# Attention of a two-layer block: padded keys, key counts inside the mask, w_out in half rows, squares on two engines

## The reference, cut to what matters

```python
proj = h @ w_in[i]
z, xbc, dt_raw, q, k, v = split(proj)
y_ssd = ssd_mixer(xbc, dt_raw, z, ...)   # ends: y = y * silu(z); y = y * rsqrt(mean(y*y per group of 256)) * ssd_norm
q = rms_norm(q per head, q_norm[i]); k = rms_norm(k per head, k_norm[i])
# three branches, dilation r in (1, 4, 16): query t sees keys t - j*r, j = 0..128
# each branch: softmax over its keys; the branches are mixed by softmax of their log denominators
y_att = dilated_attention(q, k, v)
x = x + concat([y_ssd, y_att]) @ w_out[i]
```

## Time and profile before

| | us |
|---|---|
| median of 3 runs | 2179.38 |
| lowest and highest | 2174.16, 2182.07 |
| the profiled execution | 2182.77 |
| span of its trace | 2180.8 |
| TensorE products busy | 2118.5 (97%) |
| VectorE busy | 1621.4 (74%) |
| ScalarE busy | 1132.8 (52%) |
| GpSimd busy | 441.8 (20%) |

### The profile page before, as it was taken

The page is one execution under the profiler, slowest core; times in us unless marked ns, Lnnn a source line. Parts: engine busy times, 40 slices in busy tenths (PEclk is TensorE's granted clock), DMA queues, the critical chain, the costliest instruction groups (busy, mean ns, idle before and its releaser), DMA issues. The chain is left out here.

```text
span 2180.8 us, 35065 instructions
## 1 busy us (share of the span) xinstructions
PE 2118.5 (97%) x13521; PEld 1841.5 (84%) x13521; DVE 1621.4 (74%) x2218; ACT 1132.8 (52%) x1349; POOL 441.8 (20%) x237
## 2 busy tenths in 40 slices
PE   9999999999999999999999998999989999999996
PEld 8998999569999999999559997999977777777775
DVE  5764887448657664887338565788779999999998
ACT  5333454334334343353324343524458888888885
POOL 4900180636006300090538000000000000000000
PEclk9999999999999999999999999999999999999998
DMA  8764564347556754564346653435659999999994
GB/s 268 266 205 132 165 208 150 116 164 236 179 185 203 246 192 139 161 215 146 119 139 220 200 182 97 154 116 159 228 185 374 368 374 366 366 368 377 368 368 171
DMA packets 238933, 483.82 MB, mean 222 GB/s; under 512 B 10612, under 2 KB 178976, under 8 KB 222464
## 3 DMA queue, kind: packets, MB, share of 16 engines
q1 hardware_dynamic: 226880, 443.58, 58.2%
q0 software_dynamic: 11360, 37.41, 5.2%
q10 hardware_dynamic: 608, 1.65, 0.2%
HBM read 481.50 MB, written 1.09 MB: 221 GB/s over the span
## 5 line engine op out<-in xcount | busy, mean ns | idle before, releaser
L756 PE MATMUL misc<-xh,ring_low 128*128 128x256 f32 x1472 | 410.8, 279 | 0.0
L755 PE MATMUL misc<-xl,high_b 128*128 128x256 f32 x1344 | 375.3, 279 | 0.0
L757 PE MATMUL misc<-xh,high_b 128*128 128x256 f32 x1344 | 374.7, 279 | 0.0
L2890 DVE TENSOR_TENSOR ring_low<-ring,high_b 128x2048 fp32r<-128x2048 f32 x128 | 287.2, 2285 | 0.6 <-issue 0.6
L756 PEld LDWEIGHTS misc<-xh,ring_low 128*128 128x128 f32 x1472 | 276.8, 188 | 3.3
L1729 ACT ACTIVATE arena<-arena 128x256 f32<-128x256 f32 x88 | 37.0, 420 | 429.0 <-DVE arena L2258 429.0
L755 PEld LDWEIGHTS misc<-xl,high_b 128*128 128x128 f32 x1344 | 252.3, 188 | 3.5
L757 PEld LDWEIGHTS misc<-xh,high_b 128*128 128x128 f32 x1344 | 255.1, 190 | 0.0
L1983 ACT ACTIVATE high_b<-ring 128x2048 fp32r<-128x2048 f32 x124 | 236.1, 1916 | 28.9 <-DMA ring<-in_w_dram 28.1
L2224 DVE TENSOR_TENSOR ring_low<-ring,high_b 128x2048 fp32r<-128x2048 f32 x88 | 223.3, 2574 | 15.4 <-ACT high_b L1698 15.2
L1381 PE MATMUL misc<-high_b,ue 128*128 128x512 f32 x512 | 204.2, 399 | 1.9 <-DVE ue L2933 1.2
(11 more groups left out here) (443 smaller groups left out, 5020.0 us busy)
## 6 DMA issues: line engine op xcount, KB each, us to landing
ring<-in_w_dram SPq DMA_DIRECT2D x128, 1024.0 KB, 7.8
ring<-in_w_in_dram SPq DMA_DIRECT2D x72, 1024.0 KB, 5.5
ring_d<-in_w_dram SPq DMA_DIRECT2D x128, 512.0 KB, 5.3
ring<-in_ffn_w_gate_dram SPq DMA_DIRECT2D x44, 1024.0 KB, 5.5
ring<-in_ffn_w_up_dram SPq DMA_DIRECT2D x44, 1024.0 KB, 7.9
ring_d<-in_ffn_w_down_dram SPq DMA_DIRECT2D x88, 512.0 KB, 7.5
arena<-in_w_ada_dram POOLq DMA_DIRECT2D x48, 512.0 KB, 5.0
ring<-in_w_out_dram SPq DMA_DIRECT2D x20, 1024.0 KB, 5.0
```

The costliest lines, as they stand in the source:

```text
L755: pe.matmul(dst, wh, ml, start=start, stop=False, **kw)
L756: pe.matmul(dst, wl, mh, start=False, stop=False, **kw)
L757: return pe.matmul(dst, wh, mh, start=False, stop=stop, **kw)
L2890: dve.tensor_tensor(ring_low[:, s, :], ring[:, s, :], high_b[:, s, :].bitcast(F32), ALU.subtract)\
```

## The change

The turned k goes to a new place, `keys2`, over `xc`. It holds each group of 128 channels twice: once with the rows of the odd head zero, once with those of the even head zero. ScalarE writes the zeros ahead of v block 3, when `off` has read `xc`. The scores are then products over all 128 rows, with q as it lies. Of the four banks of turned k, ScalarE empties the first two and VectorE the last two, each bank in two pieces of 64 partitions.

The mask holds 8 * log(count) where it held 0. The exponential is taken with scale 1/8, so the count comes out as a factor. ScalarE's exponentials also give the sums. `weights`, its table and `p_ready` are gone, and TensorE's transposes wait for the exponentials.

`w_out` units 0 to 13 are taken in order and in halves of 512 outputs, two or one per step by `HALVES`. Of the SSD squares, ScalarE takes the four of token tile 0 ahead of v block 3, and VectorE the four of tile 1 behind the gate.

```diff
-UNITS = {0: 0, 1: 1, 2: 2, 3: 3, 4: 4, 7: 5, 8: 8, 9: 9, 11: 6, 12: 10, 13: 11, 15: 7, 16: 12, 18: 13}
+HALVES = (2, 2, 1, 2, 1, 2, 1, 1, 2, 1, 2, 1, 2, 1, 2, 1, 2, 1, 1)
...
+    mask = np.where(cnt > 0, np.log(np.maximum(cnt, 1.0)) * HD ** 0.5, NEG)
...
+        keys2 = xc.rearrange("p (e k) s -> p e k s", e=2)
...
 # TensorE
-                    rows64 = slice(h % 2 * HD, h % 2 * HD + HD)
-                    q, k = (turned_qk(part_, h // 2)[rows64, :] for part_ in range(2))
+                    q, k = turned_q(h // 2), keys2[:, h % 2, h // 2, :]
...
-                    pe.wait_ge(p_ready, HEADS * l + h + 1)
+                    pe.wait_ge(p_exp, HEADS * l + h + 1)
...
+                rows_left = iter([(k, c) for k in range(14) for c in range(2)])
...
-                    if h in UNITS:
-                        mm = out_rows(UNITS[h])
-                        if UNITS[h] % 2:
-                            mm.then_inc(freed[(n0 + UNITS[h] // 2) % SLOTS], 1)
+                    for k, c in itertools.islice(rows_left, HALVES[h]):
+                        mm = out_rows(k, [c])
+                        if k % 2 and c:
+                            mm.then_inc(freed[(n0 + k // 2) % SLOTS], 1)
...
 # ScalarE, in the loop over the v blocks
+                    if j == 3:
+                        wait_filled(act, FILL["off", l] + 1)
+                        flat_keys = keys2.rearrange("p e k s -> p (e k s)")
+                        act.activation(flat_keys[HD:P, 0:KD * SEQ], ident[HD:P, 0:1].to_broadcast([HD, KD * SEQ]),
+                                       ACT.Copy)
+                        act.activation(flat_keys[0:HD, KD * SEQ:], ident[0:HD, HD:HD + 1].to_broadcast([HD, KD * SEQ]),
+                                       ACT.Copy)
+                        act.wait_ge(gated, l + 1)
+                        for g in range(GROUPS):
+                            ins = act.activation(xdt[:, 0, g * BLK:(g + 1) * BLK], xtok[:, 0, g * BLK:(g + 1) * BLK],
+                                                 ACT.Square, accum_out=gs[:, g:g + 1])
+                        s = step(ins)
+                        act.wait_ge(act_step, s)
                     block_out(FILL["v", l, j], 12 + j, v[:, :, j * BLK:(j + 1) * BLK])
...
-                for t in range(NT):
-                    act.wait_ge(gated, 2 * l + t + 1)
-                    for g in range(GROUPS):
...
+                act.wait_ge(sq_ready, 2 * l + 2)
                 act.activation(gss, gs, ACT.Sqrt, scale=1.0 / BLK, bias=eps).then_inc(std_ready2, 1)
...
+                for q in range(2):
+                    m = FILL["qkt", l] + 4 + q
+                    wait_filled(act, m)
+                    for e in range(2):
+                        hs = slice(e * HD, (e + 1) * HD)
+                        ins = act.mul(keys2[hs, e, 2 * q:2 * q + 2, :],
+                                      bank_of(m)[hs, :].rearrange("p (a b) -> p a b", a=2), cola[hs, l, C_KN:C_KN + 1])
+                    ins.then_inc(drained[m % 4], 1)
...
 # VectorE
+                dve.tensor_tensor(xtok[:, 0, :], xtok[:, 0, :], z[:, 0, :], ALU.mult).then_inc(gated, 1)
+                link(dve.tensor_tensor(xtok[:, 1, :], xtok[:, 1, :], z[:, 1, :], ALU.mult))
+                for g in range(GROUPS):
+                    of = xtok[:, 1, g * BLK:(g + 1) * BLK]
+                    ins = dve.tensor_tensor_reduce(xdt[:, 1, g * BLK:(g + 1) * BLK], of, of, 1.0, 0.0, ALU.mult, ALU.add,
+                                                   gs[:, GROUPS + g:GROUPS + g + 1])
+                ins.then_inc(sq_ready, 1)
...
+                for q in range(2, 4):
...
+                        ins = dve.tensor_scalar(keys2[hs, e, 2 * q:2 * q + 2, :],
+                                                bank_of(m)[hs, :].rearrange("p (a b) -> p a b", a=2),
+                                                cola[hs, l, C_KN:C_KN + 1], None, ALU.mult)
+                    ins.then_inc(drained[m % 4], 1)
...
-                def weights(h):
-                    dve.wait_ge(p_exp, HEADS * l + h + 1)
-                    dve.tensor_tensor_reduce(sp3[:, h % 3, 0:P], sp3[:, h % 3, 0:P], konst[:, K_CNT:K_CNT + P],
-                                             1.0, 0.0, ALU.mult, ALU.add, den[:, 2 * h:2 * h + 1])
...
-                        .then_inc(p_ready, 1)
```

More of the change, by code:

```diff
@@ L70 @@
 N_COLC = CONV_W * NC2
-K_ID, K_TRI, K_NEG, K_CNT, K_IOTA = 0, 128, 256, 640, 1024
-N_CONST = 1088
+K_ID, K_TRI, K_MASK, K_IOTA = 0, 128, 256, 640
+N_CONST = 704
 def constants():
@@ L86, in constants @@
     iota = np.broadcast_to(np.arange(CAP) + 1.0, (P, CAP))
-    return np.ascontiguousarray(np.concatenate(out + [np.where(cnt > 0, 0.0, NEG), cnt, iota], 1).astype(np.float32))
+    mask = np.where(cnt > 0, np.log(np.maximum(cnt, 1.0)) * HD ** 0.5, NEG)
+    return np.ascontiguousarray(np.concatenate(out + [mask, iota], 1).astype(np.float32))
 def pair_masks():
@@ L435, in two_blocks @@
         p_exp = sem("p_exp")
-        p_ready = sem("p_ready")
         av_done = sem("av_done")
@@ L1835, in ssd_and_projections @@
                                            ACT.Copy).then_inc(drained[m % 4], 1)
-                for t in range(NT):
-                    act.wait_ge(gated, 2 * l + t + 1)
-                    for g in range(GROUPS):
[L1839 to L1842, removed]
-                act.activation(gss, gs, ACT.Sqrt, scale=1.0 / BLK, bias=eps).then_inc(std_ready2, 1)
[L1844 to L1850, removed]
+                act.wait_ge(sq_ready, 2 * l + 2)
+                act.activation(gss, gs, ACT.Sqrt, scale=1.0 / BLK, bias=eps).then_inc(std_ready2, 1)
+                for q in range(4):
+                    m = FILL["qkt", l] + q
+                    wait_filled(act, m)
+                    act.mul(qk[:, :, q * SEQ:(q + 1) * SEQ], bank_of(m).rearrange("p (a b) -> p a b", a=2),
+                            cola[:, l, C_QN:C_QN + 1]).then_inc(drained[m % 4], 1)
+                for q in range(2):
+                    m = FILL["qkt", l] + 4 + q
+                    wait_filled(act, m)
+                    for e in range(2):
[3 more added lines that the diff above has]
+                    ins.then_inc(drained[m % 4], 1)
             def attention(l):
@@ L2478, in ssd_and_projections @@
                     link(dve.tensor_tensor(xtok[:, 1, cs], xtok[:, 1, cs], o, ALU.add))
-                for t in range(NT):
-                    dve.tensor_tensor(xtok[:, t, :], xtok[:, t, :], z[:, t, :], ALU.mult).then_inc(gated, 1)
+                dve.tensor_tensor(xtok[:, 0, :], xtok[:, 0, :], z[:, 0, :], ALU.mult).then_inc(gated, 1)
[5 more added lines that the diff above has]
+                ins.then_inc(sq_ready, 1)
                 dve.wait_ge(std_ready2, 2 * l + 2)
@@ L2485, in ssd_and_projections @@
                                   ALU.mult).then_inc(ysd_ready, 1)
+                for q in range(2, 4):
+                    m = FILL["qkt", l] + 4 + q
+                    wait_filled(dve, m)
+                    for e in range(2):
+                        hs = slice(e * HD, (e + 1) * HD)
+                        ins = dve.tensor_scalar(keys2[hs, e, 2 * q:2 * q + 2, :],
+                                                bank_of(m)[hs, :].rearrange("p (a b) -> p a b", a=2),
+                                                cola[hs, l, C_KN:C_KN + 1], None, ALU.mult)
+                    ins.then_inc(drained[m % 4], 1)
             def attention(l):
@@ L2504, in maxima, with attended @@
                                       ALU.mult).then_inc(smax_ready, 1)
[L2506 removed]
+                def attended(h):
                     dve.wait_ge(p_exp, HEADS * l + h + 1)
[L2508 to L2516 removed]
                     link(dve.reciprocal(rden[:, 2 * h:2 * h + 2], den[:, 2 * h:2 * h + 2]))
@@ L2527, in attention @@
                         maxima(h)
-                    if 1 <= h <= HEADS:
-                        weights(h - 1)
                     if h == 2:
```

26 lines of the change are left out of this document (11 added, 15 removed).

## The result

| | before | after |
|---|---|---|
| median of the runs, us | 2180.73 (4 runs) | 2145.14 (4 runs) |
| lowest and highest | 2174.16, 2182.23 | 2144.05, 2147.34 |
| profiled execution, span | 2182.77, 2180.8 | 2146.17, 2144.3 |

The ratio of after to before is 0.9855, with a 95% interval of 0.9826 to 0.9883: 31.6 us less, between 25.5 and 37.9. The forecast was 17.6 us less. The profiled pair differs by 36.5 us in span. The kernel before varies more from run to run than the kernel after: in 45 other executions of it, recorded beside the experiments, the mean granted clock lies between 0.984 and 0.992 (0.992 to 0.993 in the four after), and the profiled one has 0.987. One more took 5418 us and is left out of every ratio.

What follows compares the result with a forecast made beforehand. TensorE is busy 97% of the span, so time could come only from its waits or lower clock. 13.8 + 5.7 - 0.9 - 1.0 = 17.6 us off gave 2165.2 profiled, median 2161.8; range 2154 to 2171.

Steps and rivals of the forecast that it cites:

- (c): Attention scores: products over 128 rows instead of 64 cost 0, at most 0.4 us.
- (b): Attention loops: w_out in half units adds five groups a layer, 0.9 us lost, bounds 0 to 2.
- (e): Attention loops: GpSimd's hold stays on VectorE's maxima scaling and a reciprocal, 1.0 us lost, from 0 to 12.
- (a): Attention loops: TensorE's waits and low clock at steps 6, 7 and 11 go, gain 13.8 us, ends 0 to 15.
- The forecast's cover: Attention loop: turned weights are read about 4.9 us after scores begin, against a 3.2 us chain, leaving 1.7 us.
- Rival B: Attention loops: GpSimd's hold on maxima scaling replaces the masking product's, costing 8 to 18 us; gain 0 to 9; chance 0.06.
- (d): Stage ahead of each loop: squares and k emptying split between ScalarE and VectorE, gain 5.7 us, 2 to 8.
- (f): Order of loads: w_out's last load and the next feed-forward's first go out earlier; 0 gain.
- A: In or just ahead of the loop the clock falls again once or twice; gain 8 to 14; 0.19 together with another rival.
- C: Attention loops: evenly spread light work lowers the clock, up to 74 us longer, 2188 to 2236; chance 0.03.

Runs made afterwards that it cites:

- before_pad: Kernel before with only zero-padded k and scores over 128 rows, ScalarE emptying all k banks in half-partition pieces: 2166.1 us, ratio 0.9955.
- rows64: Kernel after, with scores read over the 64 rows of their head again, all else as changed: 2156.72 us, ratio 0.9932.
- the splits: Three runs of the kernel after, scores as three 128-column products with 0, 2 or 4 row-range changes per head: 2148.7, 2160.15, 2172.69 us.
- whole_units: Kernel after, with w_out in whole units at the steps of before instead of halves: 2151.87 us, ratio 0.9894.
- product_back: Kernel after, with VectorE's product by the key counts, its sums and its queue place restored: 2152.71 us, ratio 0.9876.
- before_quiet: Kernel before with GpSimd's modulation products cut from 1024 columns to 2, modulation left incomplete: 2175.15 us, ratio 0.9998.
- split_half: Kernel after, scores as three 128-column products, all over 64 rows, two row-range changes per head: 2160.15 us, ratio 0.9928.
- stage_back: Kernel after, with all eight SSD squares and all four k banks on ScalarE again: 2157.15 us, ratio 0.9893.
- split_mixed: Kernel after, scores as three 128-column products over 64, 128, 64 rows, four row-range changes per head: 2172.69 us, ratio 0.9988.

## Why the prediction was wrong, point by point

**The step that failed is (c), "Scores over 128 rows ... Cost 0".** It compared the duration of one product with that of another, 376 to 378 against 379 ns, and that comparison was right: 379 to 382 now. What the durations don't hold is the time ahead of a weight load when the number of rows changes. Twice per head there is such a change, into the scores and out of them: 2 x 0.17 = 0.34 us, 32 heads, 10.9 us. The cost had been counted in the 1.94 us of a step without a unit and left there; such a step takes 1.60 us in `before_pad`. Of the 12.9 us by which the loops beat the forecast, these are 10.9; the other two are the losses of (b) and (e), which did not come.

**(a) Waits in the loop: size right, causes in part others.** Loop gain without the 10.9 us is 24.8 - 10.9 = 13.9 us, and the forecast was 13.8. That is no independent agreement. The forecast read the stalls from the trace that the loops are compared with, and the loops after have none, so they had to come out alike. Another execution of the kernel before may hold other stalls. TensorE's waits at the transposes (L1065) were 5.0 us of them, in five waits. Most of the rest is the clock, at 0.50 for 6.8 us once in layer 0 and twice in layer 1, each time behind or within a wait of 1.1 to 1.2 us. By the runs, in us for layers 0 and 1:

| part | layer 0 | layer 1 | from |
|---|---|---|---|
| padding, the form itself | 5.4 | 5.4 | steps of 5.43 and 5.09, `rows64`, the splits |
| padding, stalls shifted and low clock that doesn't come, net | 1.9 | 5.1 | `before_pad` less the line above |
| half units | 2.1 | 2.1 | `whole_units` |
| count product | 1.3 | 1.3 | `product_back` |
| sum | 10.7 | 13.9 | measured 10.7 and 14.1 |

So about half of (a) was already gone with the padding alone, before the waits were touched; as said above, that may be a matter of how the steps lie against GpSimd's work. The first two lines are taken from the kernel before and the last two from the kernel after. That they add up is a check on the sizes. It is no proof that each would be the same in another order: `before_quiet` removed the stalls that `whole_units` and `product_back` speak of, and the whole time shows no gain from it.

**(b) Half units 0.9 us lost: no.** From the first w_out product of a step to the next scores lie 3.49 us in the kernel after (403.61 to 407.10), exactly what a unit adds (5.09 less the 1.60 of `before_pad`), where the earlier trace rows had 3.58. In `rows64` the scores start 0.52 us after the last w_out product has started, in the kernel after 0.43. So the 0.09 us was no price of a half unit but a piece of the price of the change of rows, which (c) had put at nothing. A half unit adds 1.77 us to a step of 1.60 (`before_pad`) and 1.72 to one of 3.37: no loss at a boundary is to be seen.

**(e) GpSimd's hold, 1.0 us: hit, and hidden.** The scaling of the maxima is hit harder than before:

```profile
L2532 DVE TENSOR_SCALAR arena<-arena x32: 169/564/1519, 381.9 to 1093.4; 128x2 f32<-128x2 f32 x32
```

The median is 564 ns where the earlier trace rows have 171, yet TensorE waits for nothing in the loop beyond the 0.5 us at the first w_out product. The forecast's cover was 1.7 us for steps of 3.7; for steps of 3.37 the same sum gives 1.4. The longest hold added 1.35 (1.52 less 0.17), so it just held. That was in part luck. None of these instructions began in the first 0.9 us of GpSimd's two-input product, while the count product did, at 0.04 us into it, when it took 2.58 (416.57 against 416.53 in the earlier trace rows). Rival B, with its 2.4 us, was not put to the test. Nor does a hold always last as long as GpSimd's instruction, as the forecast had it: behind the one-input product of 2.85 us, 8 of these ended after 1.15 us.

**(d) The stage: mechanism right, 4.6 us for 5.7,** mostly by the price of the half-partition pieces. **(f)** is not to be seen in any wait of TensorE in loops and stages.

**The rivals.** A did not come, and C went the other way. Steps with half a unit, ten to a layer, keep a clock of 1.00 with the padding. (Of the two light steps that the forecast held against C, step 15 holds a unit, so only one was light.) In `rows64` the clock fell with these steps in place, in step 2 (6.5 us against 4.8 in layer 1), while TensorE was busy throughout:

```profile
391.00:392.00 1.00, 1.00 (x10) 1.00 (x11) 0.81 (x5) 0.12 (x1) 0.00 (x0) 1.00 0.54 49
392.00:393.00 1.00, 1.00 (x9) 1.00 (x9) 0.00 (x0) 0.86 (x4) 0.00 (x0) 0.77 0.90 360
393.00:394.00 1.00, 1.00 (x4) 0.85 (x4) 0.17 (x1) 0.24 (x1) 0.83 (x1) 0.50 1.06 438
```

Over all traces here, the clock falls inside 6 of 10 loops with 64-row scores: in the two of the kernel before behind a wait, in four others (both of `before_quiet`, layer 0 of `rows64` and of `split_half`) in step 2 with TensorE busy throughout. In the 14 loops with scores over 128 rows none begins, though in both layers of `before_pad` and layer 1 of `stage_back` a low clock of the stage lasts 1.0 to 2.7 us into the loop. This is an association. `split_mixed` changes rows most often and had no fall in either loop, so the changes alone don't explain it, and no run takes it further.

**The rest.** Loops and stages make 29.4 us. The interval of 25.5 to 37.9 holds them. Of the profiled pair's other 7, about 4 are the two lengths of a feed-forward, and 2.5 are layer 0's projections, 177.2 against 174.7 us. The length goes with the granted clock. These projections took 174.7 to 175.5 us in the five traces whose clock stays at 1.00 between 202 and 212 us, 176.4 to 177.2 in the five with one fall of 3.4 us there, and 178.8 and 179.2 in the two with 6.9 us. Kernels with scores over 64 and over 128 rows are in the first two groups alike, so this is not put down to the change.

**The range** took no gain above 25.4 us. Its lower end had been set from the waits alone. The bounds of (c), 0 and 0.4 us of loss, were the ones that should have been wide. No row of the kernel before showed scores over 128 rows between products over 128 rows, so nothing ruled out a gain there.

## What to carry to other kernels

When small TensorE products over 64 rows stand between products over 128, count the changes of row range as well as the products: in fp32 each took 0.17 to 0.20 us here, and zero rows that make them all alike cost no product time. They cost two fills of 1.91 us, which fitted into idle time of ScalarE, and half-partition copies, which made each stage 3.2 to 3.7 us longer until VectorE took half of them and half of the squares. To price a step, compare from the start of one group to the start of the next, weight loads included, not the durations of products. A stall removed may not show in the whole time if the clock then falls elsewhere, so try the removals together and read the granted clock in slices of one microsecond.

## What the runs showed of the hardware

- A change between products over 64 and over 128 rows: 0.17 to 0.20 us, nearly linear in the number of changes (0, 2, 4 give steps of 3.39, 3.72, 4.12 us), with 0.76 us of idle ahead of the weight load instead of 0.24.
- The granted clock fell to the 1.2 GHz level with TensorE busy 1.00, at 400 us in `before_quiet` and at 392 to 393 us in `rows64`, each time about the transposes that follow 64-row scores and sixteen one-column products. The kernel after has the same order of products with 128-row scores, and stayed at 1.00. The cause is open.
- VectorE's scaling of 2 columns, 0.17 us undisturbed, took up to 1.52 us beside GpSimd. All 18 of the kernel after that took over 0.3 us end at one of three points: 1.15 us or 2.88 us after the start of GpSimd's one-input product (2.85 us long), or 2.37 to 2.39 us after that of its two-input product (2.35 us long).
- The same feed-forward of 1357 products, at clock 1.00, takes 187 or 191 us, and both lengths occur within one execution. The cause is open.
